# Block 1's feed-forward inputs: 512-column products of the rounded weights, summed by the vector engine

## The reference

```python
def swiglu(u, w1, w3, w2):
    return (jax.nn.silu(u @ w1) * (u @ w3)) @ w2

def first_block(x, c, w_in, ...):
    h = layer_norm(x)
    for l in range(DEPTH):                       # DEPTH = 2
        ada = (c_act @ w_ada[l] + b_ada[l])[:, None, :]
        sh1, sc1, g1, sh2, sc2, g2 = jnp.split(ada, 6, axis=-1)
        ...
        h = layer_norm(DN_ALPHA * h + g1 * y, ln1_g[l], ln1_b[l])
        u = h * (1.0 + sc2) + sh2
        y = swiglu(u, w1[l], w3[l], w2[l])       # w1, w3: 1024 x 2816, w2: 2816 x 1024
        h = layer_norm(DN_ALPHA * h + g2 * y, ln2_g[l], ln2_b[l])
```

## Time and profile before

| what | value |
|---|---|
| median of 3 runs | 2020.94 us (2018.0 to 2023.94) |
| span of the profiled execution | 2003.2 us |
| PE busy | 1908.6 us, 95%, 15766 matmuls |
| PE's weight loads busy | 1827.1 us, 91% |
| DVE busy | 1413.9 us, 71% |
| ACT busy | 1046.7 us, 52% |
| chain that ended last | PE 81%, DVE 10%, ACT 4% |
| of it line 476 into `projected` | 35% |

### The profile page before, as it was taken

How to read it: one execution, slowest core, us unless ns; L and a number is a source line. 1 busy time by engine, 2 the same in 40 slices (tenths; PEclk the granted TensorE clock), 3 DMA queues, 4 the chain that set the end, 5 groups by cost and what they waited for, 6 DMA issues and landing times.

```text
span 2003.2 us, 37350 instructions
## 1 busy us (share of the span) xinstructions
PE 1908.6 (95%) x15766; PEld 1827.1 (91%) x15766; DVE 1413.9 (71%) x2543; ACT 1046.7 (52%) x1611; POOL 22.2 (1%) x36
## 2 busy tenths in 40 slices
PE   5999999999999999999999999999999999999998
PEld 5999989999999998889999989878999988789998
DVE  7776576678667875676675558986666589866665
ACT  3564465444445743555444445566555445655554
POOL 1100000000002000000000000000000000000000
PEclk7999999999999999999999999999999999999999
DMA  8555544548663455455475535333455343324552
GB/s 325 185 181 202 203 162 155 205 164 318 255 238 128 179 211 189 157 184 190 142 278 199 198 107 214 142 106 106 165 199 193 128 168 132 122 89 165 189 194 102
DMA packets 52770, 358.98 MB, mean 179 GB/s; under 512 B 5995, under 2 KB 8651, under 8 KB 9980
## 3 DMA queue, kind: packets, MB, share of 16 engines
q1 hardware_dynamic: 52476, 356.54, 49.4%
q10 hardware_dynamic: 128, 0.07, 0.0%
HBM read 355.41 MB, written 1.08 MB: 178 GB/s over the span
## 4 chain that ended last, share of the span: by engine, by line
PE 81%; DVE 10%; ACT 4%; issue 2%; DMA 2%; SPq 0%; DVEq 0%; ACTq 0%
PE projected L476 35%; PE projected L1515 18%; PE mixed L476 7%; PE mixed L1515 6%; PE projected L1533 3%; DVE W L2056 2%; DVE w_lo L1457 1%; PE mixed L631 1%; DVE w_lo L393 1%; DMA w_mod<-in_first_ada_dram 1%; PE mixed L1638 1%; PE mixed L528 1%; PE mixed L1627 1%; PE mixed L1612 1%; PE mixed L552 1%
## 5 line engine op out<-in xcount | busy, mean ns | idle before, releaser
L393 DVE TENSOR_TENSOR w_lo<-raw,w_hi 128x1024 fp32r<-128x1024 f32 x340 | 409.3, 1226 | 213.8 <-ACT w_hi L736 212.7
L736 ACT ACTIVATE w_hi<-raw 128x1024 fp32r<-128x1024 f32 x338 | 349.7, 1057 | 298.8 <-PE projected L476 251.3
L476 PE MATMUL projected<-u_hi,w_hi 128*128 128x256 f32 x1728 | 486.3, 281 | 5.5 <-DVE w_lo L393 2.8
L476 PE MATMUL projected<-u_lo,w_hi 128*128 128x256 f32 x1728 | 480.3, 278 | 0.0
L476 PE MATMUL projected<-u_hi,w_lo 128*128 128x256 f32 x1728 | 480.3, 278 | 0.0
L476 PEld LDWEIGHTS projected<-u_hi,w_hi 128*128 128x128 f32 x1728 | 326.8, 189 | 12.7 <-issue 10.2
L1457 DVE TENSOR_TENSOR w_lo<-raw,w_hi 128x1024 fp32r<-128x1024 f32 x204 | 246.3, 1223 | 115.6 <-ACT w_hi L1789 115.6
L476 PEld LDWEIGHTS projected<-u_lo,w_hi 128*128 128x128 f32 x1728 | 325.5, 188 | 0.0
L476 PEld LDWEIGHTS projected<-u_hi,w_lo 128*128 128x128 f32 x1728 | 325.2, 188 | 0.0
L1515 PE MATMUL projected<-u_hi,w_hi 128*128 128x256 f32 x992 | 278.3, 281 | 7.7 <-DVE u_lo L1983 7.1
L1789 ACT ACTIVATE w_hi<-raw 128x1024 fp32r<-128x1024 f32 x204 | 211.8, 1056 | 132.1 <-PE projected L1515 113.3
(11 more groups left out here) (381 smaller groups left out, 3839.0 us busy)
## 6 DMA issues: line engine op xcount, KB each, us to landing
raw<-in_stream_dram SPq DMA_DIRECT2D x324, 1024.0 KB, 4.9
w_mod<-in_first_ada_dram SPq DMA_DIRECT2D x8, 1024.0 KB, 15.0
band<-bias_rows SPq DMA_DIRECT2D x1, 3072.0 KB, 14.3
x<-in_xT_dram SPq DMA_DIRECT2D x1, 1024.0 KB, 4.8
out_dram<-uf SPq DMA_DIRECT2D x4, 256.0 KB, 2.5
tri<-in_tri_dram SPq DMA_DIRECT2D x2, 384.0 KB, 4.3
c<-in_c_dram SPq DMA_DIRECT2D x1, 512.0 KB, 6.7
mask<-in_mask_dram SPq DMA_DIRECT2D x1, 384.0 KB, 25.6
```

The costliest lines, as they stand in the source:

```text
L393: eng.tensor_tensor(part(w_lo, step, half), raw_half(step, half), part(w_hi, step, half).bitcast(F32), ALU.subtract).then_inc(s_lo_dve, 1)
L476: m = pe.matmul(out, a, b, start=start and n == 0, stop=stop and n == 2, **kw)
L736: act.activation(part(w_hi, step, half), raw_half(step, half), ACT.Copy).then_inc(s_hi, 1)
```

## The change

u_hi and u_lo become the two parts of one tensor, `u_both`. For w1 and w3 the new `project_wide` gives each half of the chunk a bank of its own: w_hi is multiplied by both parts side by side in 512 columns, and w_lo by u_hi is added to the second 256 of them. So a chunk now takes two of the four rotating banks, and two matmuls for each half and kt in place of three. DVE adds the two 256-column parts of each bank (`whole`, two TENSOR_REDUCEs a chunk), for w1 into `sth` and for w3 into `hf`. ACT's silu then works in place in SBUF, and waits for DVE's sum; the multiplication is in place in `hf`. The banks are free when DVE has its sums.

```diff
--- before.py
+++ after.py
@@ -157,7 +157,8 @@
 CHUNKS1 = [s for s in PLAN1 if s[0] in WEIGHTED]
 MAIN1 = [s for s in CHUNKS1 if s[0] not in MODULATION]
 HELD1 = [("w2", FP * l + FP - 1) for l in range(DEPTH - 1)] + [("wo", 4 * l + 3) for l in range(DEPTH)]
-ROTATED1 = [s for s in PLAN1 if s[0] in ROTATING + ("ml_values", "ml_turn")]
+ROTATED1 = [r for s in PLAN1 if s[0] in ROTATING + ("ml_values", "ml_turn")
+            for r in ((s, (s[0] + "_second", s[1])) if s[0] in ("w1", "w3") else (s,))]
 
 
 def keep_busy(pe, out, ident, count):
@@ -185,6 +186,7 @@
     PB, MB = k["PB"], k["MB"]
 
     raw, w_hi, w_lo, u_hi, u_lo, weights_at = (k[n] for n in ("raw", "w_hi", "w_lo", "u_hi", "u_lo", "weights_at"))
+    u_both = k["u_both"]
     vecs = sb("vec", [P, DEPTH, V_END])
     wgate = sb("wgate", [P, DEPTH, KT, 16])
     wgate_hi = sb("wgate_hi", [P, KT, 16], F32R)
@@ -335,6 +337,7 @@
     s_tab = sem("mask_and_distances_landed")
     s_scaled = sem("last_norm_scaled")
     s_bank = sem("output_bank_done")
+    s_whole = sem("feed_forward_sum_ready")
 
     NB = [MB, PB]
 
@@ -369,11 +372,11 @@
 
     def taken(step):
 
-        kind, N, l, i = local(step)
+        kind, N, l, i = local((step[0].removesuffix("_second"), step[1]))
         return {"qk": (s_zc, N + 1), "v": (s_v, N + 1), "aq": (s_qkv, 18 * l + i + 1),
                 "ml_values": (s_mtk, N + 1), "ml_turn": (s_hm, N + 1), "ak": (s_qkv, 18 * l + i + 7), "av": (s_qkv, 18 * l + i + 13), "o": (s_tho, 12 * l + i + 1),
                 "gbr": (s_tho, 12 * l + i + 5), "wa": (s_mix, 6 * l + i + (1 if i < 2 else 3)), "wo": (s_pre, 16 * l + 2 * i + 2),
-                "w1": (s_th, N + 1), "w3": (s_hf, N + 1)}[kind]
+                "w1": (s_whole, 2 * N + 1), "w3": (s_whole, 2 * N + 2)}[kind]
 
     ADAS = [s for s in CHUNKS1 if s[0] in MODULATION]
 
@@ -501,6 +504,25 @@
                                 skip_group_check=True)
                     if kt == KT - 1:
                         m.then_inc(s_used, 1)
+
+        def project_wide(step, ready=None):
+
+            outs = bank(step), bank((step[0] + "_second", step[1]))
+            slot = MAIN1.index(step) % SPLIT
+            hi, lo = (w[:, slot, :].rearrange("p (h k n) -> p h k n", h=2, k=KT) for w in (w_hi, w_lo))
+            order = [(kt, half) for kt in range(KT) for half in range(2)] if ready is not None else \
+                    [(kt, half) for half in range(2) for kt in range(KT)]
+            if ready is not None:
+                split(step, 1)
+            for kt, half in order:
+                if ready is None and kt == 0:
+                    split(step, half)
+                if ready is not None and half == 0:
+                    pe.wait_ge(s_u, ready + kt + 1)
+                pe.matmul(outs[half][:], hi[:, half, kt, :], u_both[:, :, kt, :], start=kt == 0, stop=False)
+                m = pe.matmul(outs[half][:, T:2 * T], lo[:, half, kt, :], u_hi[:, kt, :], start=False, stop=kt == KT - 1)
+                if kt == KT - 1:
+                    m.then_inc(s_used, 1)
 
         def project_tokens(step, x):
             out = bank(step)
@@ -678,10 +700,7 @@
                 m.then_inc(s_var, 1)
                 keep_busy(pe, MB[3], ident, 8)
             elif kind in ("w1", "w3"):
-                if kind == "w1" and i == 0:
-                    project_first(step, (u_hi, u_lo), 16 * l + 8)
-                else:
-                    project(step, (u_hi, u_lo))
+                project_wide(step, 16 * l + 8 if kind == "w1" and i == 0 else None)
             elif kind == "w2":
                 pe.wait_ge(s_hid, N + 1)
                 if i == 0:
@@ -876,11 +895,8 @@
                 act.wait_ge(s_hf, N + 1)
                 act.activation(hid_hi[:, 2 * i:2 * i + 2, :], hf[:], ACT.Copy).then_inc(s_hidh, 1)
             elif kind == "w1":
-                b = result(step)
-                if i >= 2:
-                    act.wait_ge(s_hid, N - 1)
-                act.activation(sth[i % 2][:], PB[b][:].rearrange("p (a t) -> p a t", a=2), ACT.Silu)\
-                   .then_inc(s_th, 1)
+                act.wait_ge(s_whole, 2 * N + 1)
+                act.activation(sth[i % 2][:], sth[i % 2][:], ACT.Silu).then_inc(s_th, 1)
 
     def vector(dve):
         steps = k["dve_steps"]
@@ -921,6 +937,14 @@
 
         def halves(ap):
             return ap.rearrange("p (a t) -> p a t", a=2)
+
+        def whole(step, to):
+
+            dve.wait_ge(s_used, done(step))
+            for half, part in enumerate((step, (step[0] + "_second", step[1]))):
+                out = PB[turn(part)][:].rearrange("p (b t) -> p t b", b=2)
+                ins = dve.tensor_reduce(to[:, half, :], out, AX, ALU.add)
+            ins.then_inc(s_whole, 1)
 
         def scale_and_shift(vec, g, b, part):
             r = rstd[:].rearrange("p (o t) -> p o t", o=1).to_broadcast([P, part.stop - part.start, T])
@@ -1181,12 +1205,15 @@
                     for kt in range(KT):
                         ins = dve.tensor_scalar(hT[:, kt, :], cen[:, kt, :], vec[:, b + kt:b + kt + 1], None, ALU.add)
                     link(ins)
+            elif kind == "w1":
+                whole(step, sth[i % 2])
             elif kind == "w3":
-                b = result(step)
-                dve.wait_ge(s_th, N + 1)
                 if N:
                     dve.wait_ge(s_hidh, N)
-                dve.tensor_tensor(hf[:], sth[i % 2][:], halves(PB[b][:]), ALU.mult).then_inc(s_hf, 1)
+                whole(step, hf)
+                dve.wait_ge(s_th, N + 1)
+                dve.wait_ge(s_whole, 2 * N + 2)
+                dve.tensor_tensor(hf[:], sth[i % 2][:], hf[:], ALU.mult).then_inc(s_hf, 1)
                 dve.wait_ge(s_hf, N + 1)
                 dve.wait_ge(s_hidh, N + 1)
                 dve.tensor_tensor(hid_lo[:, 2 * i:2 * i + 2, :], hf[:], hid_hi[:, 2 * i:2 * i + 2, :].bitcast(F32),
@@ -2337,8 +2364,8 @@
         k["w_hi"] = sb("w_hi", [P, SPLIT, CHUNK], F32R)
         k["w_lo"] = sb("w_lo", [P, SPLIT, CHUNK], F32R)
         sb("gap_u", [P, (behind(k["weights_at"], nc.sbuf_base, 64) - nc.sbuf_base) // 4])
-        k["u_hi"] = sb("u_hi", [P, KT, T], F32R)
-        k["u_lo"] = sb("u_lo", [P, KT, T], F32R)
+        k["u_both"] = sb("u_both", [P, 2, KT, T], F32R)
+        k["u_hi"], k["u_lo"] = k["u_both"][:, 0], k["u_both"][:, 1]
         k["base"] = -(-nc.sbuf_base // 32) * 32
 
         first = first_block(nc, ctx, A, hT, k)
```

## The result

The changed kernel takes 2032.41 us (median of six executions, 2027.07 to 2040.99); six executions of the kernel before, the first three among them, gave 2019.47 (2013.88 to 2023.94). The ratio is 1.0094, 95% interval 1.0059 to 1.0128: slower by 19 us, between 12 and 26; the two medians themselves lie 12.9 us apart, near the low end. The direction was forecast and 2032.41 lies in the range, but the size is two to three times the 6 us forecast. The profiled execution of after took 2027.07 with a span of 2025.3, so 1.8 us lies around a span. Its span is 22.1 longer than the 2003.2 of before.

A forecast was written before the change was run, and what follows sets the result against it. The prediction took DVE to bound the head of each feed-forward and PE the body. Layer 0's +4.6 and layer 1's +1.4 made +6.0 us on 2020.94, a forecast of 2027.0 us, range 2020 to 2034.

The forecast's parts named there:

- a triple becomes 216 + 113 = 329 ns: PE in w1 and w3: one 512-column and one 256-column matmul replace three of 256, 329 ns instead of 340.
- a 256-column matmul waits for the next load about as much as for its own columns. A matmul twice as long hides it: PE in w1 and w3: a load takes 0.11 us, like the matmul gap, so 512 columns would take 216 ns.
- Rival 2: PE in w1 and w3: the wide matmul saves nothing, total 2032 us; chance 0.20 together with a dear reduce.
- -3.1 a layer: PE's saving in each layer's feed-forward: 18 half-rounds (w1 or w3 chunks) at 0.173 us less each.
- TENSOR_REDUCE at 0.68 and 1.28 a pair: DVE's new sums after each w1 and w3, priced by elements read: 1.28 us a pair until the result.
- rival 1: DVE's heads and rounds: the reduce is priced by what it writes, a pair 0.7 us, total 2019.5; chance 0.20.
- The head: Start of each feed-forward: the sums delay silu, the rounding of w3(1) and hf, so w2(0) starts 2.9 us later.
- Rival 3: Both feed-forwards: all the DVE work hides, only PE's 7.6 us saving counts, total 2013 us; chance 0.05.
- the late starts after the head: PE waits for DVE's weights: +1.3 us in each layer, +3.2 in layer 0's two rounds with two modulations.
- DVE's 17.6 us round: Layer 0's rounds with two modulations: DVE needs 17.6 us including sums and pauses, against PE's forecast 15.97.
- The end: Last chunk of each feed-forward: the pair of sums delays hf, so w2(10) starts late, +0.4 us with the restart.
- 17.7 more, which lies around the span and stays: Whole kernel: the timed median 2020.94 exceeds the profiled span 2003.2 by 17.7 us, taken as unchanged time outside the span.

The follow-up runs named there:

- wide_wide: The changed kernel with w_lo also multiplied by both parts of u, so no narrow matmul is left in w1 and w3; 2097.34 us, one execution.
- contiguous: The changed kernel with u_both laid out so a wide matmul's 512 columns are one stretch in SBUF; 2038.41 us, ratio 1.011 against the kernel before.
- wide_no_sum: The changed kernel without DVE's sums: silu and multiplication read only each bank's first 256 columns; 2021.66 us, ratio 1.0027 against the kernel before.
- narrow: The changed kernel with each 512-column matmul split into two of 256, sums and waits kept; 2027.63 us, ratio 1.0061 against the kernel before.
- silu_behind: The changed kernel with ACT's silu of w1 issued behind the rounding of the next weights; 2027.67 us, ratio 1.007 against the kernel before.

## Why the forecast was wrong, step by step

**The step that failed** is "a triple becomes 216 + 113 = 329 ns", and behind it "a 256-column matmul waits for the next load about as much as for its own columns. A matmul twice as long hides it". The first wide matmul behind a stream at the short rate takes 0.226 and those in a mixture 0.235, in each case exactly two narrow ones, and in wide_wide they take 0.231 and 0.236. What holds a narrow one therefore grows with its columns; had it been the wait for the next load, the wide one would have been shorter than two. There was nothing to hide. The load's 0.11 and the matmul's 0.113 were two things of about equal length, and the rows could not tell which was the bound; the earlier trace rows is of another kind of data (plain fp32), its matmuls have 256 columns and not 512, and it was taken as the nearest. Its 216 ns is thus no confirmation of 216 for 512 columns, as the prediction read it; no fp32r matmul of 512 columns came below 0.225 in a stream.

Rival 2, "the wide matmul saves nothing", had the right consequence, but its reason, "if the second source stretch or the wide write costs what the load gave", is refuted for the stretch by contiguous; nothing had to be given back. And it stopped at no gain (340): the mixture does worse, 353 (the long rate for all 768 columns). Instead of -3.1 a layer the term is +5.8 against a body at the short rate, and, before's own bodies being slow three times in eight, +3.6 against the average one.

**What the sum gives now.** Against the first profile 22.7 (12.3 + 10.4), near the 22.1 of the spans (in part luck, since the matmuls outside the bodies draw their rates too); against the average execution of before 3/8 x 11.5 = 4.3 less, 18.4, where 19 [12, 26] was measured (12.9 between the medians). For wide_no_sum, without the 11.2 us of waits in the table, 7.2 (measured 5 [1, 10]); for narrow, the 11.2 alone (12 [7, 18]); for contiguous 18.4 again (22 [12, 33]); for silu_behind, whose feed-forwards are 1.0 and 1.4 shorter, 18.4 - 2.4 = 16.0 (14 [9, 19]). These agree within what is measured, but they lean on a share counted in eight bodies.

**Right:** TENSOR_REDUCE at 0.68 and 1.28 a pair (rival 1 refuted); by the 1x mode that the Trainium skill gives it ("VectorE: DVE Perf Modes", the perf-mode tier table), 512 elements at that page's 0.96 GHz are 0.53 us, an estimate, and the pitch of 0.60 in the pair agrees with a price by what is read. The head: +2.9 forecast, 3.1 and 3.0 measured, by the forecast path of silu, rounding and second pair, which silu_behind and wide_no_sum confirm. Rival 3, all DVE work hides, is refuted by the same. Layer 0's rounds with two modulation chunks wait (18.71 and 17.09), layer 1's second round (16.96) does not.

**Off in size:** the late starts after the head, 1.3 + 3.2 forecast in layer 0 and 2.75 measured, 1.3 and 0.9 in layer 1. PE's round was 16.96 and not 15.97, so that DVE's 17.6 us round exceeded it by less. The end was +0.4 and is +0.5, with 0.2 more for w2(9) at the long rate. From the start of w2(0) on, +1.7 and -1.5 were forecast for the two layers; +9.2 and +7.3 were measured.

**Wrong beside it:** "17.7 more, which lies around the span and stays". It is 1.8. The profile of before was a short execution (its bodies both at 113.3), and the median an average over draws. The base for a median was right all the same, since 2020.94 was used, but the profile was that of a better than average before, and the forecast never asked why an execution should be 16 us shorter than the median.

**Open:** what in TensorE makes the two rates, and why a mixture of widths always ended in the longer one. The traces show narrow ones changing the rate at a pause (the waits in narrow) and where the streamed operand goes from weights to u; a cause is not shown for either.

## What to carry to other kernels

When a matmul's pitch and its load are equally long, a row cannot say which one bounds it: look for a row of the same type at another width before booking a saving. Ahead of any gain of a few ns per instruction, profile the kernel before more than once: if a stage repeats exactly within an execution and differs between executions, the gain can vanish in that, and the profile at hand may be its best draw. A sum moved to the engine that already prepares the next weights costs its full length at each head, and once more for what stands behind the engine that waits for it.

## What the hardware showed that was not expected

- Streams of fp32r matmuls have one of two exact rates at the same granted clock (1.00): 113.3 or 117.8 ns per 256 columns. In the bodies of before the one taken behind a pause held for all of some 1380 narrow matmuls. Within a stretch without a pause it turned at 31 of 32 changes from streamed weights to streamed u, so a rate is not drawn at pauses alone.
- Mixed 512- and 256-column matmuls ran at 117.8 in ten bodies of ten, also in the two (wide_no_sum) where they followed without a pause on a stream at 113.3. 512-column ones alone alternated between 231 and 236 ns.
- This alone makes two executions of the kernel before differ by 19 of their 21 us.
